# First transformer block of a fused two-block kernel: output chunk split inside the attention, second norm rows in two instructions, next layer's first row turned inside the last FFN products

## What is computed

```python
for i in range(DEPTH):                    # DEPTH = 2
    h = rmsnorm(x, norm1_g[i])
    mix = hybrid_mixer(h, w_in[i], ...)   # 21 attention units and a compressed branch
    x = x + mix @ w_out[i]
    h = rmsnorm(x, norm2_g[i])
    x = x + conv_glu_ffn(h, w_up[i], conv_w[i], conv_b[i], w_down[i])
return rmsnorm(x, final_g)                # then the second block starts on it
```

## Time and profile before

| | |
|---|---|
| median of three runs | 1961.68 us (1961.12 to 1968.07) |
| time of the profiled execution | 1960.8 us |
| its span, first to last instruction | 1959.0 us |
| TensorE busy | 1857.9 us, 95% of the span |
| VectorE busy | 1360.4 us, 69% |
| ScalarE busy | 954.4 us, 49% |
| mean granted TensorE clock | 0.984 of full |

### The profile page before, as it was taken

One profiled execution on the slowest core, in us unless ns is written; L12 is line 12 of the kernel. 1 busy time (PEld: TensorE's weight loads), 2 busy tenths in 40 slices (PEclk: granted clock), 3 DMA queues, 4 the chain that ended last, 5 costly groups with the idle time before them and its releaser, 6 DMA issues.

```text
span 1959.0 us, 31245 instructions
## 1 busy us (share of the span) xinstructions
PE 1857.9 (95%) x12538; PEld 1705.0 (87%) x12538; DVE 1360.4 (69%) x2157; ACT 954.4 (49%) x1413; POOL 99.3 (5%) x104
## 2 busy tenths in 40 slices
PE   7998999899899989999999999998999999999997
PEld 5887999788799989998988889997999888979997
DVE  4476778647677877767777777677666776765455
ACT  5556444545654455344655354444443664444432
POOL 0000000000000000000002201100000001400100
PEclk9999999999999999999999999998999999999999
DMA  7215777531367767775430257775775442035552
GB/s 275 71 66 194 286 280 273 189 116 66 129 258 281 279 237 272 278 283 192 168 134 23 86 204 283 297 277 214 280 282 210 150 135 85 1 129 194 193 202 77
DMA packets 54509, 374.42 MB, mean 191 GB/s; under 512 B 6016, under 2 KB 6656, under 8 KB 12800
## 3 DMA queue, kind: packets, MB, share of 16 engines
q1 hardware_dynamic: 51536, 361.98, 50.4%
q0 software_dynamic: 2304, 9.93, 1.3%
q10 hardware_dynamic: 560, 0.99, 0.2%
HBM read 371.83 MB, written 1.05 MB: 190 GB/s over the span
## 4 chain that ended last, share of the span: by engine, by line
PE 85%; DVE 8%; ACT 5%; issue 2%; DMA 0%; ACTq 0%; SPq 0%; DVEq 0%
PE bank L688 14%; PE bank L690 13%; PE bank L689 13%; PE bank L837 6%; PE bank L838 6%; PE bank L839 6%; PE bank L754 3%; PE bank L755 3%; PE bank L756 3%; PE bank L1297 2%; DVE w_lo L1909 2%; PE bank L1307 1%; ACT w_hi L1395 1%; PE bank L799 1%; PE bank L1010 1%
## 5 line engine op out<-in xcount | busy, mean ns | idle before, releaser
L1909 DVE TENSOR_TENSOR w_lo<-raw,w_hi 128x2048 fp32r<-128x2048 f32 (+4 forms) x273 | 604.8, 2219 | 85.3 <-ACT w_hi L1395 85.1
L688 PE MATMUL bank<-hT_hi,w_hi 128*128 128x256 f32 x2304 | 654.1, 284 | 2.0 <-DVE scratch L2615 2.0
L689 PE MATMUL bank<-hT_lo,w_hi 128*128 128x256 f32 x2304 | 651.8, 283 | 0.0
L690 PE MATMUL bank<-hT_hi,w_lo 128*128 128x256 f32 x2304 | 651.8, 283 | 0.0
L1395 ACT ACTIVATE w_hi<-raw 128x2048 fp32r<-128x2048 f32 (+4 forms) x270 | 505.4, 1875 | 146.3 <-PE bank L839 116.2
L688 PEld LDWEIGHTS bank<-hT_hi,w_hi 128*128 128x128 f32 x2304 | 440.1, 191 | 8.9 <-issue 6.5
L689 PEld LDWEIGHTS bank<-hT_lo,w_hi 128*128 128x128 f32 x2304 | 440.2, 191 | 2.8 <-issue 0.5
L690 PEld LDWEIGHTS bank<-hT_hi,w_lo 128*128 128x128 f32 x2304 | 440.2, 191 | 0.2
L837 PE MATMUL bank<-w_hi,hid_hi 128*128 128x512 f32 x528 | 206.7, 391 | 3.4 <-DVE w_lo L1909 2.7
L838 PE MATMUL bank<-w_lo,hid_hi 128*128 128x512 f32 x528 | 206.2, 390 | 0.0
L839 PE MATMUL bank<-w_hi,hid_lo 128*128 128x512 f32 x528 | 205.4, 389 | 0.0
(11 more groups left out here) (401 smaller groups left out, 2396.4 us busy)
## 6 DMA issues: line engine op xcount, KB each, us to landing
raw<-in_wb SPq DMA_DIRECT2D x158, 1024.0 KB, 4.8
raw<-in_wa SPq DMA_DIRECT2D x94, 1024.0 KB, 4.9
scratch<-in_wm SPq DMA_DIRECT2D x72, 1024.0 KB, 7.0
raw<-in_wb SPq DMA_DIRECT2D x8, 940.0 KB, 4.6
raw<-in_wb SPq DMA_DIRECT2D x4, 936.0 KB, 4.5
lnw<-in_ln_g POOLq DMA_DIRECT2D x6, 512.0 KB, 4.5
lnw<-in_ln_b POOLq DMA_DIRECT2D x6, 512.0 KB, 5.7
scratch<-in_c SPq DMA_DIRECT2D x5, 512.0 KB, 3.7
```

The source lines that it names most:

```text
L688: nc.tensor.matmul(out, ah, bh, start=(i == 0), stop=False)
L689: nc.tensor.matmul(out, ah, bl, start=False, stop=False)
L690: last = nc.tensor.matmul(out, al, bh, start=False, stop=(i == n - 1))
L1909: return nc.vector.tensor_tensor(w_lo[:, slot, cols], raw[:, raw_slot, cols], w_hi[:, slot, cols].bitcast(F32), ALU.subtract)
```

## The change

There are six edits. (1) The high part of the first output chunk is made in four quarters of 512 columns, one behind each of the attention's steps 17 to 20 on ACT; its low part is one DVE instruction at the end of step 20. (2) `second_row(1)` writes the norm in two instructions, each with the four blocks of one bank, and TensorE turns a bank when its half is there. (3) `final_row(1)` does the same by halves of 512 columns. (4) In layer 0, TensorE turns the next layer's row 0 in the sweep's last quarter, ahead of its last three matmuls. (5) ACT does row 1's first square ahead of row 0's split, and both engines split two blocks of row 0 instead of four ahead of row 1's norm; DVE adds row 1's second half ahead of any split. (6) Counts of `xn` go from four to five a layer, with the waits that use them, and three unused semaphore names go.

```diff
 PER_A = {
     "zero": 6, "tp": 12, "blk": 11, "ix": 8, "s": 21, "pt": 21, "o": 21, "ckv": 1, "cs": 1, "cpt": 1, "co": 1,
     "tp_hi": 32, "pj": 11, "blk_ev": 10, "dup": 4, "ix_relu": 8, "gate_e": 1, "e": 21, "pt_ev": 21, "cg_e": 1,
-    "dila_e": 1, "cexp": 1, "cpt_ev": 2, "ss": 6, "std": 2, "rstd": 4, "xn": 4, "tp_lo": 32, "rope_i": 1, "rope_h": 1,
+    "dila_e": 1, "cexp": 1, "cpt_ev": 2, "ss": 6, "std": 2, "rstd": 4, "xn": 5, "tp_lo": 32, "rope_i": 1, "rope_h": 1,
     "rw": 2, "gate": 1, "ix_acc": 8, "keys": 1, "nm": 21, "o_ev": 8, "cg": 1, "cgel": 1, "ckv_ev": 1, "dila": 1,
     "cnm": 1, "cp": 1, "x": 8,
 }
...
         start_in, small_in, out_st = sem("start_in"), sem("small_in"), sem("out_st")
         gain_in = sem("gain_in")
         ln_in = sem("ln_in")
-        FIN = {n: sem("fin_" + n) for n in ("rstd", "x")}
+        FIN = {n: sem("fin_" + n) for n in ("rstd", "x_half", "x")}
         NEXT = {n: sem("next_" + n) for n in ("ss", "std")}
 
         A = {n: sem("a_" + n) for n in (
...
                 for v, b in zip(dil_zones, (T_KW, T_KW, T_AQ + 2)):
                     pool.wait_ge(A["blk"], due(A, "blk", b // 2 + 1))
                     nc.gpsimd.memset(v, 0.0).then_inc(A["zero"], 1)
-                pool.wait_ge(A["xn"], 2 * TT * l + 2 * TT)
+                pool.wait_ge(A["xn"], due(A, "xn", 2 * TT + 1))
                 pool.dma_start(lnw[:, 0, :], t["gain"][l + 1, :].partition_broadcast(P)).then_inc(gain_in, 16)
                 if l + 1 < DEPTH:
-                    pool.wait_ge(A["xn"], 2 * TT * l + 3 * TT)
+                    pool.wait_ge(A["xn"], due(A, "xn", 3 * TT + 1))
             for l in range(DEPTH):
                 layer["first"] = l
                 for sub in range(3):
...
 
                 turn_row(i, lambda half: pe.wait_ge(B[f"nx{i}"], due(B, f"nx{i}", 2 * sub + half + 1)))
 
-            def turn_tile(N, src, i, run):
+            def turn_tile(N, src, i, run, ready=lambda bank: None):
 
                 for bank in range(2):
+                    ready(bank)
                     for k in range(KT):
                         if turn_bank(k, run) == bank:
                             last = nc.tensor.transpose(turn_at(i, k, run), src[:, i, k * P:(k + 1) * P], ident)
...
                     nc.tensor.matmul(GATE[sub][half][:, :], const("ones"), gdiag[:, 4 * half:4 * half + 4, :].rearrange("p k n -> p (k n)"),
                                      start=True, stop=True).then_inc(B["gateb"], 1)
 
-            def ffn(N, split, h0, v, gate=None):
-
+            def ffn(N, split, h0, v, gate=None, turn_first=None):
 
                 def up(f, f2, pos, slot, wait_bank=True, features=None):
                     pe.wait_ge(lo_done, pos + (1 + NEW) + split)
...
                     for i, half, part_of in ((0, 0, tiles[:3]), (0, 1, tiles[:2]), (0, 0, tiles[3:]), (0, 1, tiles[2:]),
                                              (1, 0, tiles), (1, 1, tiles)):
                         for f, f4, k2, slot in part_of:
+                            if (i, half, f) == (1, 1, FT - 1) and turn_first is not None:
+                                turn_first()
                             if (i, half) == (0, 0):
                                 if f == FT - 2:
                                     pe.wait_ge(lo_done, FFN_N - 1 + (1 + NEW) + split)
...
                 layer["first"] = l
                 split = l * A_S
 
-                pe.wait_ge(A["xn"], due(A, "xn", 1))
-                turn_tile(A, xn, 0, 1)
+                if l == 0:
+                    pe.wait_ge(A["xn"], due(A, "xn", 1))
+                    turn_tile(A, xn, 0, 1)
+
+                def turn_next():
+
+                    pe.wait_ge(A["xn"], due(A, "xn", 2 * TT + 2))
+                    turn_tile(A, xn, 0, 1)
 
                 def turn_second():
 
...
                 token_pair(G, [(A_WIN + c) % RING for c in (2, 3)],
                            lambda half: pe.wait_ge(lo_done, split + (A_WIN + 2 + half + 1 + NEW)),
                            lambda i: pe.wait_ge(A["x"], due(A, "x", i + 1)), turn_first)
-                pe.wait_ge(A["xn"], due(A, "xn", 2 * TT))
-                turn_tile(A, xn, 1, 2)
-                ffn(A, split + (A_WIN + A_WOUT), FT * l, 2)
+                turn_tile(A, xn, 1, 2, lambda bank: pe.wait_ge(A["xn"], due(A, "xn", 2 * TT + bank)))
+                ffn(A, split + (A_WIN + A_WOUT), FT * l, 2, turn_first=turn_next if l + 1 < DEPTH else None)
 
 
             pe.wait_ge(start_in, 16)
...
                 layer["first"] = l
                 split = l * B_N + S_A
                 for i in range(TT):
-                    turn_row(i, lambda half, i=i: pe.wait_ge(FIN["x"], TT * l + i + 1))
+                    if i and l == 0:
+                        turn_row(i, lambda half: pe.wait_ge(FIN["x"], TT) if half else pe.wait_ge(FIN["x_half"], 1))
+                    else:
+                        turn_row(i, lambda half, i=i: pe.wait_ge(FIN["x"], TT * l + i + 1))
                 ffn(B, split, FT * (DEPTH + 2 * l), 0, gate=0)
                 gate_on_all(1)
                 turn_normal(0, 0)
...
                     act.wait_ge(small_in, 16)
                     hi_tile(A, 0, 0, "g1")
                 else:
-                    hi_tile(A, 0, 0, "g1", range(0, 4))
-                    rms_tile(NEXT, 1, 6 * l + 3, lambda i, half: act.wait_ge(A["x"], summed(l - 1, i, half)))
-                    hi_tile(A, 0, 0, "g1", range(4, KT))
+                    act.wait_ge(A["x"], summed(l - 1, 1, 0))
+                    square(NEXT, 1, 0)
+                    half_mean(NEXT, 1, 6 * l + 4)
+                    hi_tile(A, 0, 0, "g1", range(0, 2))
+                    act.wait_ge(A["x"], summed(l - 1, 1, 1))
+                    square(NEXT, 1, 1)
+                    root_mean(NEXT, 1, 6 * l + 6)
+                    hi_tile(A, 0, 0, "g1", range(2, KT))
                 hi_tile(A, 0, 1, "g1")
                 hi_a(1)
                 def tile_out(c, i):
...
                         nc.scalar.activation(pcT4[0:32], G[1][0:32, SEQ:2 * SEQ].rearrange("p (t n) -> p t n", t=TT),
                                              ACT.Copy).then_inc(A["cpt_ev"], 1)
 
+                def hi_quarter(q):
+
+                    s_, cols = A_WIN, slice(q * CW // 4, (q + 1) * CW // 4)
+                    if q == 0:
+                        act.wait_ge(raw_in[(s_ + A_D) % RING], arrivals(l, s_ + A_D))
+                        act.wait_ge(chunk_mm, split + s_ + 1)
+                    last = nc.scalar.activation(w_hi[:, s_ % RING, cols], raw[:, (s_ + A_D) % RING, cols], ACT.Copy)
+                    if q == 3:
+                        last.then_inc(hi_done, 1)
+
                 for step in range(NU + LAG_T):
                     if step < NU:
                         exponentials(step)
                     if step >= LAG_T:
                         copy_weights(step - LAG_T)
                     compressed(step)
-                hi_a(A_WIN)
+                    if 0 <= step - NU + 4 < 4:
+                        hi_quarter(step - NU + 4)
                 hi_a(A_WIN + 1)
                 for i in range(TT):
                     hi_tile(A, 1, i)
...
                     dve.wait_ge(small_in, 16)
                     lo_tile(A, 0, 0, "g1")
                 else:
-                    lo_tile(A, 0, 0, "g1", range(0, 4))
                     sums(l - 1, 1, 1)
+                    lo_tile(A, 0, 0, "g1", range(0, 2))
                     plain_row(1, TT * l + 2, 2 * TT * l + 2)
-                    lo_tile(A, 0, 0, "g1", range(4, KT))
+                    lo_tile(A, 0, 0, "g1", range(2, KT))
                 lo_tile(A, 0, 1, "g1")
                 for c in range(1, A_WIN - 1):
                     lo_a(c)
...
                     taken = take(eight, found)
                     compressed(step)
                     dilations(step)
-                lo_a(A_WIN)
+                    if step == NU - 1:
+                        lo_a(A_WIN)
                 for i in range(TT):
                     lo_tile(A, 1, i)
 
...
                 def second_row(i):
 
                     normed(A, TT * l + i + 1, A, 2 * TT * l + TT + i + 1, i)
-                    gained_row(i, xn).then_inc(A["xn"], 1)
+                    if i == 0:
+                        gained_row(i, xn).then_inc(A["xn"], 1)
+                    else:
+                        for bank in range(2):
+                            blocks = lambda v: v.rearrange("p (a b n) -> p a b n", b=2, n=2 * P)[:, :, bank, :]
+                            nc.vector.scalar_tensor_tensor(out=blocks(xn[:, i, :]), in0=blocks(x[:, i, :]), scalar=st[:, 20 + i:21 + i],
+                                                           in1=blocks(lnw[:, 0, :]), op0=ALU.mult, op1=ALU.mult).then_inc(A["xn"], 1)
 
                 lo_a(A_WIN + 1)
                 lo_a(A_WIN + 2)
...
             def final_row(i):
 
                 normed(NEXT, TT * DEPTH + i + 1, FIN, i + 1, i)
```

(9 more changed lines are left out.)

3 lines of the change are left out of this document (1 added, 2 removed), and 1 row of the table B.

## The result

**1968.95 us median of 20 runs (1961.8 to 1981.33), against 1963.08 for the kernel before in the same number of runs beside it (1959.11 to 1972.89): the ratio is 1.003, 95% interval 1.0017 to 1.0043.** By the medians the kernel got slower by 5.9 us, 0.3%. That is less than the 0.5% that the prediction took for the least change that can be told, but the interval leaves out 1, and the median lies outside the range of 1956.0 to 1966.5. The profiled execution took 1966.32 us, 5.5 more than the profiled one before.

A forecast was written before the change was run, and what follows sets the result against it. TensorE holds 85% of the chain that ended last, so only its waits at borders between stages count. Terms +1.0 - 0.9 - 0.4 + 0.1 = -0.2 us gave a median of 1961.5 against 1961.68, range 1956.0 to 1966.5.

The forecast's parts named there:

- The queues: Attention to output products: ACT's last exponentials slip 0.54 us, DVE's low part waits for the fourth quarter, last output 1.62 later.
- The price of the queues at full clock: Attention to output products: first product at 150.60 against 150.06, taken as 0.5 us worse per layer, +1.0 for two.
- rival (b): Output products: TensorE falls to half clock at the first product, 1.7 us per layer, 1964.9 in all; chance 17%.
- The halves: Output products to FFN (twice) and first block to second: halved norm moves products 0.58 us forward, bringing 0.44 each.
- rival (c): Norm rows: their shorter stretches escape the fall to half clock, each bringing 1.7 us more, 1956.4 in all; chance 10%.
- The layer border: Layer 0 to layer 1: DVE's gain is lost to TensorE's order, +0.1 us, between 0.5 better and 0.5 worse.
- Rival (a): Attention to output products: the low part hides in DVE's idle time, each layer gains 1.1 us, 1958.3 in all; chance 15%.

The follow-up runs named there:

- experiment 3: The changed kernel with the four quarters behind steps 14, 16, 17 and 18 instead of 17 to 20: 1961.9 us, 0.9994 of the kernel before.
- 5: The changed kernel with 14 unread products a layer in TensorE's idle time in the attention's tail: 1962.92 us, 1.002 of the kernel before.
- experiment 2: The kernel before with the split of the output chunk inside the attention as its only edit: 1973.21 us, 1.005 of the kernel before.
- experiment 6: The kernel before with the norm of the second rows and of final row 1 in two instructions as its only edit: 1959.54 us, 0.999.
- experiment 7: The kernel before with only the layer border's edit (earlier turn of layer 1's first row, new order of splits and norm): 1962.15 us, 1.0011.
- 1: The changed kernel with the output chunk's split put back behind the attention on both engines: 1959.07 us, 0.9988 of the kernel before.
- experiment 8: The kernel before with quarters behind steps 14, 16, 17 and 18 and the norm halves, layer border unchanged: 1962.15 us, 1.0011 of the kernel before.
- 9: The kernel of experiment 8 with ten unread products a layer in TensorE's idle time: median 2.7 us below 11; its own time is not in the text.
- 11: The kernel of experiment 6 with the same ten unread products a layer as 9: median 2.7 us above 9; its own time is not in the text.

## Why the prediction was wrong, point by point

**The queues: right.** A quarter is 0.61 to 0.62 us, the last exponentials slip by 0.52 (forecast 0.54), VectorE idles 2.48 us ahead of the low part, and the last output is 1.47 us later where I had 1.62. Late arrival of the fourth quarter as the reason that the low part does not hide is shown by experiment 3, where earlier quarters alone hide it.

**The price of the queues at full clock: a little high.** I took 0.5 worse a layer at the first product. At the full level the sixteen transposes bring the product 1.79 us behind the last output (experiments 3 and 5), so the changed kernel without a fall would be at 11.72 + 1.79 = 13.51 against 13.24: 0.3 worse, worked out from those rows.

**The step that failed: the term of "0.5 us worse" a layer, with every duration on TensorE taken at the full level.** From the first exponential of step 18 to the start of the layer's last output sum the kernel before takes 36.79 and 36.77 us, the changed one 41.95 and 38.68: 5.2 and 1.9 us worse, and of that only 0.3 each is the queues. The clock came in only as rival (b), with the fall *at the output products*, 3.4 us long, 1.7 us a layer, 17%. In layer 1, and in both layers of experiment 2, that is what came: a fall of 3.4 us on the transposes, the first product 14.71 - 13.51 = 1.2 late and about 0.9 us of products at half rate behind it, some 1.6 in all. In layer 0 the fall lies earlier, in the attention's tail, where the instructions are small; it lasts 13.7 us, four times as long; and it slows the values, the compressed branch, the transposes and the first 2.4 us of output products, 4.9 us in all.

The reason given for rival (b) was also wrong in one number. It counts 4.2 us from the last values product to the first output product, but by the prediction's own account both slip by 0.5, which leaves 3.7, no more than before. What grew are two idle times of TensorE: ahead of the values of step 21 (1.07 against 0.55) and ahead of the transposes (1.67 against 0.73), where it stands waiting for the outputs behind the low part. The first stood in my text as "TensorE's products of step 21, and with them the end of the compressed branch, slip by the same 0.5", with nothing put against it; for the second I had the last output 1.62 late and did not ask what TensorE does until then.

The profiled executions, stretch by stretch:

```
us                                                before    changed   difference
start to layer 0's first exponential               94.54      97.47     +2.93
to that of step 18 (layer 0)                       42.27      40.63     -1.64
to the last output sum (layer 0)                   36.79      41.95     +5.16
to the first FFN product, and sixty further  5.26, 27.92  4.56, 28.62   -0.70, +0.70
first sweep sum to layer 1's first exponential     89.75      90.31     +0.56
to that of step 18 (layer 1)                       42.16      40.53     -1.63
to the last output sum (layer 1)                   36.77      38.68     +1.91
to the first FFN product, and sixty further  5.20, 27.97  4.57, 28.51   -0.63, +0.54
into the second block, and sixty further     6.06, 30.43  5.28, 31.06   -0.78, +0.63
the rest                                         1195.18    1193.61     -1.57
```

With 0.03 in the stretches left out that is the 5.5 us by which the two spans differ. The entries of 1.6 and 2.9 go with clock falls elsewhere: a longer one at the start of the changed kernel's execution, none at 91.9, 450.3 and 1692.7, where the kernel before has one each.

The Trainium skill, "TensorE: Matmul & The Clock Gate", section "HAM oscillation — how this bites in real kernels", warned of gaps between bursts of matmuls. The trace agrees in kind. The waits in the page's example are of 3 to 5 us; here idle times of 1.07 and 1.67 us went with a fall.

**One execution is not the median.** Even with the profile in hand the median has to be explained over runs: changed 1961.8 to 1981.3, in step with the mean clock, and the split alone up to 1983.7. My range took the spread of three runs of before, and I gave the change a fixed price in all executions, where a change that makes a fall likelier moves the whole lot of runs. With the clock's part taken out (0.88 of the loss in the table) the changed kernel is at 1933.1 against 1933.6 and 1933.4: a change of -0.3 to -0.5 us, where the sum of my terms at a clock left as it was said -0.2. So the sum was near, and the clock that it left out is the error.

**The halves: right, with the doubt about the clock.** A half took 0.75 us (I took 0.70). The product comes 0.7 and 0.6 us earlier at the two FFN borders and 0.8 earlier at the block border, where I had 0.44 each, since products moved forward would run at half rate. They did: of the 2.1 us 1.1 is left in experiment 6 once the level is up again, against my 1.3, and 0.2 in the changed kernel's execution, where the fall came later. The clock is low there as in the kernel before (3.4 us from 185.1 and from 543.5, 6.8 from 738.1): rival (c) did not happen.

**The layer border: right in sign.** +0.35 in the changed kernel, +0.24 alone (a part of which may be the clock's, see experiment 7), where I took +0.1 between ends of -0.5 and +0.5. TensorE's new order eats VectorE's gain, as forecast.

**Rival (a)** did not happen in the changed kernel (15%), but experiment 3 shows that four numbers in the loop decide it: 12.03, where the changed kernel would be at 13.51 at the full level.

**Open.** What decides in an execution whether the lower level lasts 3.4 or 13.7 us in the attention, or comes at all, is not settled: the kernels of experiments 1, 3, 6 and 8 have the same instructions on TensorE at the attention's beginning and differ there. The profiled layers tell where the late split's falls begin, the other runs only how much clock was lost, not where. The early quarters seem to cost some clock as well: the clock loss of experiments 3 and 8 has a mean of 35.3 us, that of their counterparts 1 and 6, which lack the early quarters, 30.5, with a standard error of 1.3 for the difference. In both their profiles the long fall lies at the attention's beginning, ahead of the quarters, and why is not known; with the fill (9 against 11) the difference is gone.

## What to carry to other kernels

An idle gap on an in-order engine can take work only if the work's input is ready when the gap opens: look up when the producer's last piece ends, and move that piece before moving the consumer, since here two or three steps' difference in the loop took the first product, at full clock, from 0.3 us late to 1.2 early in each layer. Where a change lengthens TensorE's idle times in or behind a stage of small, dependent matmuls, even by 0.5 to 1 us, read the granted clock of the stage itself and expect the time to move with it. Look at the mean clock of every run too, not only at the profile: it told here what one execution could not. If runs scatter with the mean clock, put a few unread products into TensorE's idle time at the places where the profile shows the fall: ten a layer at both places removed the longest times here, fourteen in the tail alone did not, and only with the ten did the gain show in the medians.

## What the runs showed of the hardware that I had not expected

- TensorE's lower level came in the first block in stretches of 3.4, 6.8 and 13.7 us, and one of 13.7 us lay in a window in which TensorE was busy 14.00 of 14.00 us (experiment 8). A 128x256 product of the logits took 0.63 us there and 0.38 at the full level, so a busy TensorE in a profile is not a TensorE at its rate.
- The same kernel had a mean granted clock from 0.975 to 0.984, worth 19.5 us of span. It is most of what separates one run of it from another: the standard deviation falls from 4.3 to 1.5 us with the clock's part taken out.
- Unread products cost almost nothing where TensorE idles: ten a layer moved the median of the kernel before by -0.8 us, within its interval.
- Where TensorE waited 1.07 us ahead of the values of step 21, and in three of the six layers 1.67 us ahead of the transposes too, the clock fell in five layers of six; where it waited 0.55 and 0.73 us, in none of twelve.
